# Two blocks of a transformer on one core: gate projections and convolution taps moved into the attention rounds, seven expert buffers instead of five

## The reference, cut to what matters

```python
# experts, both layers: 4 groups of 8, the best group and its 2 best experts
combine = sum(one_hot(expert_id, 32) * weights)
hid = silu(t @ w1[e]) * (t @ w3[e]) * combine[:, e]      # per expert e, 1024 -> 128
y = sum over e of hid[e] @ w2[e]                         # 128 -> 1024

# second block, per layer: four branches over the same normed input h
p = split_proj(h @ w_in)
att = softmax([q k_local / 8, q k_ctx / 8, sink]) @ [v_local, v_ctx]   # 8 heads, 2 key heads
a = att * silu(p['att_z'])                               # the gate, 512 wide
f = silu(layer_norm(depthwise_conv(glu(p['cf_glu']), 31 taps) + bias)) * silu(p['cf_z'])
```

## Time and profile before

| | us |
|---|---|
| three runs | 3669.21, 3670.17, 3674.32 (median 3670.17) |
| the profiled execution | 3664.03 |
| its span (first to last instruction) | 3662.2 |
| TensorE busy | 3361.4 (92%) |
| DVE busy | 1732.4 (47%) |
| ACT busy | 876.0 (24%) |
| loads by SP's queue | 348.01 MB, 30.1% of 16 engines' span |

### The profile page before, as it was taken

The page is one execution under the profiler, slowest core; times in us unless marked ns, Lnnn a source line. Parts: engine busy times, 40 slices in busy tenths (PEclk is TensorE's granted clock), DMA queues, the critical chain, the costliest instruction groups (busy, mean ns, idle before and its releaser), DMA issues.

```text
span 3662.2 us, 34488 instructions
## 1 busy us (share of the span) xinstructions
PE 3361.4 (92%) x12728; PEld 1956.7 (53%) x12728; DVE 1732.4 (47%) x3260; ACT 876.0 (24%) x1745; POOL 128.9 (4%) x132
## 2 busy tenths in 40 slices
PE   7987887999999787988899999999989789999998
PEld 3443553444444554544555555555544456678886
DVE  1153224546542324866634444444458664454554
ACT  2041212222331122035122121111121513222222
POOL 0000330000000230000000000000000000000000
PEclk8998998999999898989999999999999999999998
DMA  7624774667423674100111111221222021223331
GB/s 243 209 67 169 287 278 134 210 204 218 120 64 121 240 302 151 46 18 17 46 35 46 46 51 53 58 63 52 58 64 69 1 62 49 63 68 87 87 87 58
DMA packets 410644, 393.87 MB, mean 108 GB/s; under 512 B 27728, under 2 KB 353488, under 8 KB 401776
## 3 DMA queue, kind: packets, MB, share of 16 engines
q1 hardware_dynamic: 376928, 348.01, 30.1%
q10 hardware_dynamic: 15120, 23.68, 1.9%
q0 software_dynamic: 18432, 19.98, 1.6%
HBM read 440.78 MB, written 31.52 MB: 129 GB/s over the span
## 4 chain that ended last, share of the span: by engine, by line
PE 77%; DVE 9%; ACT 3%; issue 3%; DMA 2%; ACTq 0%; POOL 0%; DVEq 0%; POOLq 0%
PE psum L661 36%; PE psum L646 16%; PE psum L850 5%; DVE arena L1894 4%; PE psum L1041 3%; PE psum L869 2%; ACT arena L1361 1%; PE psum L1157 1%; PE psum L835 1%; PE psum L717 1%; DVE arena L1887 1%; PE psum L1181 1%; PE psum L1193 1%; PE psum L746 1%; DMA ring<-in_w_branch 1%
## 5 line engine op out<-in xcount | busy, mean ns | idle before, releaser
L646 PE MATMUL psum<-hT,ring 128*128 128x512 f32 (+1 forms) x1920 | 774.7, 562 | 18.0 <-DVE hT L1887 15.7
L661 PE MATMUL psum<-arena,ring 128*128 128x384 f32 (+1 forms) x2592 | 751.6, 441 | 28.0 <-ACT part_sum L1369 15.2
L661 PEld LDWEIGHTS psum<-arena,ring 128*128 128x128 f32 x2592 | 494.8, 192 | 255.5 <-ACT part_sum L1369 17.7
L661 PE MATMUL psum<-hT,ring 128*128 128x384 f32 (+1 forms) x2176 | 624.2, 440 | 4.2 <-DVE arena L1894 4.2
L646 PEld LDWEIGHTS psum<-hT,ring 128*128 128x128 f32 x1920 | 363.8, 191 | 424.1 <-issue 410.2
L661 PEld LDWEIGHTS psum<-hT,ring 128*128 128x128 f32 x2176 | 414.6, 191 | 193.5 <-issue 12.7
L1369 ACT ACTIVATE arena<-psum 128x512 f32<-128x512 f32 (+5 forms) x481 | 206.6, 467 | 602.8 <-PE psum L646 284.8
L1891 DVE TENSOR_TENSOR ring<-ring 128x512 f32<-128x512 f32 (+1 forms) x336 | 215.9, 662 | 278.4 <-PE psum L661 268.1
L1369 ACT ACTIVATE part_sum<-psum 128x384 f32<-128x384 f32 (+1 forms) x324 | 143.0, 441 | 817.3 <-PE psum L661 814.8
L1361 ACT ACTIVATE arena<-psum,cols 128x256 f32<-128x256 f32 (+3 forms) x272 | 131.0, 501 | 673.8 <-PE psum L850 277.9
L1891 DVE TENSOR_TENSOR psum<-psum,part_sum 128x384 f32<-128x384 f32 (+1 forms) x244 | 120.6, 498 | 287.8 <-PE psum L661 278.9
(11 more groups left out here) (224 smaller groups left out, 2759.3 us busy)
## 6 DMA issues: line engine op xcount, KB each, us to landing
arena<-in_moe_w SPq DMA_DIRECT2D x64, 1536.0 KB, 10.6
ring<-in_w_in SPq DMA_DIRECT2D x172, 512.0 KB, 4.0
ring<-in_ada_w SPq DMA_DIRECT2D x96, 512.0 KB, 5.5
ring<-in_ssm_w_in SPq DMA_DIRECT2D x48, 512.0 KB, 6.6
ring<-in_w_mod SPq DMA_DIRECT2D x48, 512.0 KB, 4.7
ring<-in_w_branch SPq DMA_DIRECT2D x64, 256.0 KB, 3.0
ring<-in_mix_w_in SPq DMA_DIRECT2D x16, 512.0 KB, 7.7
arena<-acs_dram ACTq DMA_DIRECT2D x32, 256.0 KB, 3.3
```

The costliest lines, as they stand in the source:

```text
L646: mm = nc.tensor.matmul(b[:, 0:n], ws[k // 8][0][:, k % 8, :], rhs(k)[:, o:o + n], start=(k == 0), stop=(k == nk - 1))
L661: mm = nc.tensor.matmul(flat(bank_, nb), lhs[:, k, :], rhs(k), start=(start and k == 0), stop=(k == kd_ - 1), skip_group_check=True)
```

## The change

It has two parts.

Experts: `HELD` goes from 5 to 7. The sixth buffer is ring slots 6 and 7 with one half of `square` (two DMAs, L1354 and L1355 of the changed kernel), the seventh is the token part of `hT`'s first six tiles (one DMA, L1357). Both are free in the expert stage once the routing product (expert 5) and the transposes of the token rows (expert 6) are done, and SP waits for those. `step_weights` finds a block by thirds. Expert e now waits for step (e - 7) // 2.

Attention of the second block: att_z is cut into 12 parts of 256 columns in layer 0 and 8 in layer 1. Two are made ahead of round 0's transposes and one in each of the following rounds, between scores and transposes; the bank is taken after the first head's scores. ACT reads each part twice (`z_part_out`): tanh into a buffer of its own, and a plain copy into `br`. DVE does 3 taps of `conv(3)` per round in layer 0 and 4 in layer 1, behind `att_max`, and multiplies a finished block's two halves there (one instruction in every third or second round). What is left behind the rounds is the four sums, the weight sums and four `z_apply`. `att_done` moves to a small memset behind them.

```diff
@@ -39,7 +39,7 @@
...
 EW = 3 * KD * P
-HELD = 5
+HELD = 7
 DEEP = 3
@@ -367,18 +367,27 @@
...
         rs_ = mE.take(12, 4)
-        held_at = MODW - HELD * EW
+        held_at = MODW - 5 * EW
         assert mE.at <= held_at
-        expert_w = [arena[:, held_at + EW * i:held_at + EW * (i + 1)] for i in (3, 4, 0, 1, 2)]
+        in_thirds = lambda t: [t[:, 0:D], t[:, D:2 * D], t[:, 2 * D:3 * D]]
+        held = [in_thirds(arena[:, held_at + EW * i:held_at + EW * (i + 1)]) for i in (3, 4, 0, 1, 2)]
+        held.append([ring[:, i].rearrange("p k n -> p (k n)") for i in (RING2, RING2 + 1)]
+                    + [square.rearrange("p a n -> p (a n)")[:, 0:D]])
+        held.append([hT[:, 2 * i:2 * i + 2, 0:S] for i in range(3)])
         spare_w = [ring[:, 3 * i:3 * i + 3, :, :].rearrange("p a k n -> p (a k n)") for i in range(2)]
...
-        def step_weights(s, h):
-            return expert_w[(2 * s + h) % HELD] if s < STATIC else spare_w[h]
+        def step_thirds(s, h):
+            return held[(2 * s + h) % HELD] if s < STATIC else in_thirds(spare_w[h])
+        def step_weights(s, h, at, n):
+            third, at = step_thirds(s, h)[at // D], at % D
+            return third[:, at:at + n] if len(third.shape) == 2 else third[:, at // S, at % S:at % S + n]
@@ -458,7 +467,16 @@
...
+            if n % 16 < 4:
+                return br_free[:, (S + L) * (n % 16):(S + L) * (n % 16 + 1)]
             return z_bufs[n % 16 // 8][:, n % 2, :]
+        Z_PART = {"x0": (0, S // 2), "x1": (S // 2, S // 2), "c": (S, L)}
+        def z_parts(l, r):
+            each = [(c, tag) for c in range(4) for tag in Z_PART if tag != "c" or l == 0]
+            return each[0:2] if r == 0 else each[r + 1:r + 2]
@@ -848,7 +866,7 @@
...
                             mm = nc.tensor.matmul(b[LANES * h:LANES * h + LANES, 0:2 * P], rowsT[:, i % 2, k, LANES * h:LANES * h + LANES],
-                                                  step_weights(s, h)[:, 2 * P * k:2 * P * k + 2 * P],
+                                                  step_weights(s, h, 2 * P * k, 2 * P),
                                                   start=(k == 0), stop=(k == KD - 1), skip_group_check=True)
@@ -1117,8 +1135,26 @@
...
-                    def att_scores(n, j):
+                    z_w = {}
+                    def z_job(c, tag):
+                        if tag == "x0":
+                            if (l, c) == (0, 0):
+                                slots.shrink()
+                            z_w[c] = take()
+                        return job("att_z", l, c, tag)
+                    def z_product(c, tag, b, full):
+                        o, w = Z_PART[tag]
+                        for k in range(KD):
+                            mm = nc.tensor.matmul(b[:, 0:w], z_w[c][0][:, k, :], hT[:, k, o:o + w], start=(k == 0), stop=(k == KD - 1))
+                        mm.then_inc(tensor_done, pe.step([full] + ([z_w[c][1]] if tag == ("c" if cx else "x1") else [])))
+                    def att_scores(n, j, z=()):
                         for hh in range(4):
+                            if hh == 1:
+                                for c, tag in z:
+                                    z_bank[c, tag] = z_job(c, tag)
                             h = 4 * j + hh
@@ -1131,10 +1167,15 @@
...
+                    z_bank = {}
                     att_scores(*rounds[0])
+                    for c, tag in z_parts(l, 0):
+                        z_product(c, tag, *z_job(c, tag))
                     for r, (n, j) in enumerate(rounds):
                         if r + 1 < len(rounds):
-                            att_scores(*rounds[r + 1])
+                            att_scores(*rounds[r + 1], z=z_parts(l, r) if r else ())
+                            for c, tag in z_parts(l, r) if r else ():
+                                z_product(c, tag, *z_bank[c, tag])
                         kt = key_tiles(n)
@@ -1157,10 +1198,6 @@
...
                         mm.then_inc(tensor_done, pe.step(full))
-                    if l == 0:
-                        slots.shrink()
-                    for c in range(4):
-                        linear(("att_z", l, c), h_, c=cx)
                     todo = pairs(l)
@@ -1304,7 +1341,20 @@
...
                         eng.wait_ge(tensor_done, sp.at(("full",) + jobname("out" + "AM"[l], 0, "x")))
-                    eng.dma_start(expert_w[e % HELD], a[f"moe_w_{l}"][e]).then_inc(expert_landed[e % HELD], sp.landing(f"expert_{e % HELD}", ("expert", l, e)))
+                    elif e == 5:
+                        eng.wait_ge(tensor_done, sp.at(("full",) + jobname("route", l)))
+                    elif e == 6:
+                        eng.wait_ge(tensor_done, sp.at(("full",) + jobname("h_tok", l, 3, 1)))
+                    w = a[f"moe_w_{l}"][e]
+                    to = held[e % HELD]
+                    if e % HELD < 5:
+                        i = (3, 4, 0, 1, 2)[e % HELD]
+                        eng.dma_start(arena[:, held_at + EW * i:held_at + EW * (i + 1)], w).then_inc(expert_landed[e % HELD], sp.landing(f"expert_{e % HELD}", ("expert", l, e)))
+                    elif e % HELD == 5:
+                        eng.dma_start(ring[:, RING2:RING2 + 2].rearrange("p s k n -> p (s k n)"), w[:, 0:2 * D]).then_inc(expert_landed[5], sp.landing("expert_5", None))
+                        eng.dma_start(to[2], w[:, 2 * D:3 * D]).then_inc(expert_landed[5], sp.landing("expert_5", ("expert", l, e)))
+                    else:
+                        eng.dma_start(hT[:, 0:6, 0:S], w.rearrange("p (k n) -> p k n", n=S)).then_inc(expert_landed[6], sp.landing("expert_6", ("expert", l, e)))
                 eng.wait_ge(tensor_done, sp.at(("step_done", l, ORDER[-1])))
@@ -1656,17 +1706,6 @@
...
-                def z_tanh(name, l, c, cx):
-                    n = zn["n"]
-                    zn["n"] += 1
-                    if n >= 2:
-                        eng.wait_ge(vector_done, ac.at(("zt_used", n - 2)))
-                    for tag, o, w in parts(cx):
-                        j = jobname(name, l, c, tag)
-                        eng.wait_ge(tensor_done, ac.at(("full",) + j))
-                        act(zt(n)[:, o:o + w], bank(j)[:, 0:w], ACT.Tanh, scale=0.5).then_inc(scalar_done, ac.step(("zt", n, tag)))
@@ -1740,10 +1779,22 @@
...
                         act(col("stat", 32 * q + 12, 4), col("stat", 32 * q + 12, 4), ACT.Exp).then_inc(scalar_done, ac.step(("es2", l, n, j)))
+                    def z_part_out(some):
+                        for c, tag in some:
+                            o, w = Z_PART[tag]
+                            j = jobname("att_z", l, c, tag)
+                            eng.wait_ge(tensor_done, ac.at(("full",) + j))
+                            act(zt(16 * l + c)[:, o:o + w], bank(j)[:, 0:w], ACT.Tanh, scale=0.5).then_inc(scalar_done, ac.step())
+                            copy(br[:, c, o:o + w], bank(j)[:, 0:w]).then_inc(scalar_done, ac.step([("free",) + j, ("att_z", l, c)]))
                     rounds = [(n, j) for n in x_tiles(l) for j in range(2)]
+                    z_part_out(z_parts(l, 0)[0:1])
                     att_exp(0, *rounds[0])
+                    z_part_out(z_parts(l, 0)[1:2])
                     for r, (n, j) in enumerate(rounds):
                         nl = len(key_tiles(n))
+                        if 0 < r < len(rounds) - 1:
+                            z_part_out(z_parts(l, r))
                         if r >= 1:
@@ -1766,8 +1817,7 @@
...
                     eng.dma_start(tabs, a["consts"][:, CONST["dplus"][0]:CONST_W - ROUTE_W]).then_inc(tabs_landed, ac.landing("tabs", ("tabs", l)))
-                    for c in range(4):
-                        z_tanh("att_z", l, c, cx)
+                    zn["n"] += 4
@@ -2529,16 +2572,17 @@
...
-                    def conv(c):
-                        eng.wait_ge(vector_done, ve.own())
+                    def conv(c, k0=0, k1=32):
                         acc = br[:, 8 + c, 0:w_]
-                        ts(acc, cu[:, c % 2, 0:w_], cw(0, c)).then_inc(vector_done, ve.step())
-                        for k in range(1, 31):
+                        for k in range(k0, min(k1, 32)):
                             eng.wait_ge(vector_done, ve.own())
-                            stt(acc, cu[:, c % 2, k:k + w_], cw(k, c), acc, ALU.mult, ALU.add).then_inc(vector_done, ve.step(("cu_free", l, c + 2) if k == 30 else None))
-                        eng.wait_ge(vector_done, ve.own())
-                        ts(acc, acc, 0.5, V("cf_conv_b_2", 4 * l + c), ALU.mult, ALU.add).then_inc(vector_done, ve.step(("cf_conv", l, c)))
+                            if k == 0:
+                                ts(acc, cu[:, c % 2, 0:w_], cw(0, c)).then_inc(vector_done, ve.step())
+                            elif k < 31:
+                                stt(acc, cu[:, c % 2, k:k + w_], cw(k, c), acc, ALU.mult, ALU.add).then_inc(vector_done, ve.step(("cu_free", l, c + 2) if k == 30 else None))
```

(19 more changed lines are left out.)

17 lines of the change are left out of this document (5 added, 12 removed).

## The result

The changed kernel takes 3611.45 us (median of four runs, 3603.64 to 3614.83), where the kernel before, measured beside it, takes 3669.69. The ratio is 0.9843 with the interval 0.9825 to 0.9861, so 58 us were gained (51 to 64). The forecast was 3581, a gain of 90. Direction and range hold; a third of the size is missing. The profiled execution took 3612.57 us, its span is 3610.8.

A forecast was written before the change was run, and what follows sets the result against it. TensorE was taken as the longest chain almost everywhere, idle in the expert stages and second block's attention. 3664.03 - 53 (experts) - 37 (attention) = 3574 us profiled; the median lies 6.1 higher, so 3581 was forecast, range 3560 to 3622.

The forecast's parts named there:

- The unhindered step: Expert loop: a step without stalls takes 6.45 us, so the 21 steps of a stage take 135.5 us.
- Experts with seven buffers: Expert stages: weight latency covered, 379 GB/s needed, TensorE bounds with about 9% in hand; gain 28 + 25 = 53 us.
- The term that failed: Expert stages: 3 us per stage kept as lost to late odd spare step weights and bursts beside row traffic.
- The prediction's own sign of being wrong: Expert stages: experts' loads still stall TensorE over 10 us a stage; the other sign was rounds off 14.3 by over 1.
- Rival (b): Expert stages: rate stays at 299 and 302 GB/s, some 10 us gained in both, 3623 us; chance 0.11 with half-way case.
- Rival (c): Expert loop: y-row scatter lands late beside the full queue, stretching every step; 3757 us; 0.03 with anything like it slower.
- The rounds: Second block's attention: rounds go from 12.5 to 14.3 us, TensorE with ACT the bound; round 1 taken as 13.0.
- Behind the rounds: After the last attention round starts: 21.2 us in layer 0, 21.7 in layer 1, with some 11 us of idle TensorE.
- Rival (a): Attention rounds: gate parts absorbed with little lengthening because the clock stays up; about 15 us better, 3566; chance 0.12.
- (d): Attention rounds: gate parts delay the exponentials, 17 us a round in layer 0, part 2 gives nothing; 3617; chance 0.07.
- The sum: Whole kernel: 53 us from the experts and 37 from the attention, forecast median 3581 us.
- The range: Whole kernel: 3560 to 3622 us, holding the forecast with both bounds, (a), (d) and most of (b).

## Why the prediction was right in direction and too large in size

- **The unhindered step.** Right: 6.45 us, 135.5 for the stage, reached exactly when the spare loads are out.
- **Experts with seven buffers.** Right that no up product of a static step waits any more, and right on the rate: 391 GB/s were sustained. The Trainium skill's 358 GB/s (DMA: Bandwidth & Descriptors, Specifications) would have cost 8 us more per stage. The same page says, in Measured, that a core gets about that much when both cores of a pair stream, and this kernel runs on one core; the measured mean lies above it for 85 us, so the trace was the better guide.
- **The term that failed** is "I keep 3 us per stage as lost", with its reason, "weights of the odd spare step ... may still be late, once or twice". Measured: six waits a stage, 14.3 and 12.9 us in sum, and 158.89 - 135.5 = 23.4 and 19.3 us lost, the slower clock behind the waits included. The 3 us had no row behind them. The trace of before held what was needed: hardly anything waited for the spare weights, but they were used 6.55 to 8.2 us after their issue, in a period that the forecast itself shortened from 23.8 to 19.35 us. The prediction asked what a faster TensorE collides with for experts and for y rows, but not for the third load of the loop. This is 37 of the 53 us by the profile, 32 by the ratio of the seven buffers alone. The prediction's own sign of being wrong, experts' loads that stall TensorE for over 10 us a stage, came in this form: not the loads of the 32 experts, but POOL's loads of spare weights.
- **Rival (b)**, bandwidth, came closer in size (some 10 us gained in both stages, measured 16 to 20) for the wrong reason. Its sign was a rate that stays at 299 and 302 GB/s, and it came: 294 and 299. But a rate that doesn't rise shows only that no more was asked for.
- **Rival (c)**, the y scatter stretching every step, didn't show: no step waited for rows or row buffers.
- **The rounds.** Right within 0.3 us from round 3 on (14.57 against 14.3 where all three key tiles are seen). Wrong in rounds 1 and 2. Round 1 was taken as 13.0 us and took 17.0 in layer 0 and 15.4 in layer 1; round 2 took 15.2. In round 1 of layer 0 the granted clock was 0.90 in the mean, the gate product took 5.38 us (at 0.69) and not 3.7, and in both layers TensorE waited 1.01 us for DVE there. Round 0 was 2.1 us shorter than taken. So the last round started at 147.2 us after the first scores where 143.3 was forecast, and in layer 1 at 106.0 for 102.5.
- **Behind the rounds.** Right: 20.7 and 21.6 us where 21.2 and 21.7 were summed, with the new stall of 10.62 and 10.82 released by ACT's copy.
- **Rival (a)** (rounds at about their old length) and **(d)** (17 us rounds) fell with the 14.57.
- **The sum.** 16 + 31 = 47 by the windows, 52 by the two parts' ratios, 58 by the whole's, against 90. The first two differ from the last by no more than runs of one kernel do at the start of the kernel and in the stages. (The terms as written add up to 3580, not 3581.)
- **The range** held, but not for its reasons. The result lies outside the 3568 to 3596 that had the chance 0.66, and in the range 3560 to 3622 only because rivals (b) and (d) had widened it. The case that came, a loop of spare loads, was none of the rivals; that its cost fell among theirs is luck.

## What to carry to other kernels

When a wait is to be removed from a loop, list every other load of that loop and measure for each the time from issue to use, not only whether someone waits. A load that is used 7 us after its issue and needs 6 is invisible until the loop gets 4 us shorter, and then it is the bound. Take such a load away for one run, as here, and the run tells at once whether anything else stands behind it. Before you issue it earlier, look at what stands ahead of it in its own queue, since it may only wait there longer. And where work is moved off a tail that two engines share, move it off both: the end waits for whichever queue is left.

## What was not expected of the hardware

A gather by POOL whose rows are all out of bounds brings no weights, but it isn't free: it still puts 144 packets of 4 bytes into POOL's queue and takes its place there. It landed within 2.7 us of the second issue with no expert in flight, 5 to 7 us after the first issue beside them, 7.7 to 9.0 when issued earlier (all in layer 0), and with three times as many the up product came 9.3 us after the last issue of its part. Beside the experts' loads a scatter issued into an empty POOL queue also started only 4.4 us after its issue, against 1.5 without them. On the other side, a single core sustained 391 GB/s in the mean of 85 us, 20 of the 33 MB in rows of 12 KB, beside the row traffic, with slices up to 443.
